# MLP input split beside the merge's output tiles, norm roots behind the up products, one ring of weight parts

## The reference, cut to what matters

```
x = x + g1 * merge_branches(ya, yb, pg, up_a, up_b, out_w)
#   merge: (sigmoid(pg_a) * (ya @ up_a) + sigmoid(pg_b) * (yb @ up_b)) @ out_w
x = x + g2 * squared_relu_mlp(modulate(rms_norm_2(x, norm2_w), sh2, sc2), mlp_w1, mlp_w2)
#   modulate(v, sh, sc) = v * (1 + sc) + sh
#   squared_relu_mlp(h, w1, w2) = square(relu(h @ w1)) @ w2          w1: 2048 x 8192
return rms_norm_2(x, final_norm_w)
```

## Time and profile before

| what | value |
|---|---|
| median of 3 runs | 4190.42 us |
| profiled execution: its time, its span | 4188.9 us, 4186.9 us |
| TensorE busy | 3830.8 us, 91% of the span |
| VectorE, ScalarE, GpSimd busy | 2062.7 (49%), 1522.9 (36%), 1636.1 us (39%) |
| mean granted TensorE clock, as a share of 2.4 GHz | 0.952 |
| HBM traffic | 139 GB/s over the span |
| stage C, first to last matmul | 3199.8 to 3392.7 us |
| up and down products of stage M | 3403.3 to 4173.0 us |

### The profile page before, as it was taken

The page is one execution under the profiler, slowest core; times in us unless marked ns, Lnnn a source line. Parts: engine busy times, 40 slices in busy tenths (PEclk is TensorE's granted clock), DMA queues, the critical chain, the costliest instruction groups (busy, mean ns, idle before and its releaser), DMA issues. The chain is left out here.

```text
span 4186.9 us, 86156 instructions
## 1 busy us (share of the span) xinstructions
PE 3830.8 (91%) x37360; PEld 3518.3 (84%) x37360; DVE 2062.7 (49%) x3724; ACT 1522.9 (36%) x2656; POOL 1636.1 (39%) x1160
## 2 busy tenths in 40 slices
PE   7898999898899899999879888898898979999998
PEld 6788887788888788888768778787787979999998
DVE  2544433533334677677665555556554443333333
ACT  3333343333344442232223333333333444444443
POOL 1544553444454553333311111111113636666664
PEclk9999998999999999999979999999997989999999
DMA  4354443344443677778500000000004535555553
GB/s 159 131 183 150 167 177 133 130 171 151 152 161 141 205 270 266 252 253 291 193 22 20 25 25 25 6 22 25 6 2 157 192 111 186 181 182 182 189 181 134
DMA packets 115670, 587.20 MB, mean 140 GB/s; under 512 B 20832, under 2 KB 40160, under 8 KB 50528
## 3 DMA queue, kind: packets, MB, share of 16 engines
q1 hardware_dynamic: 115296, 581.71, 39.0%
HBM read 560.95 MB, written 20.71 MB: 139 GB/s over the span
## 5 line engine op out<-in xcount | busy, mean ns | idle before, releaser
L536 PE MATMUL bank<-act_L,part_L 128*128 128x256 f32 x7296 | 968.5, 292 | 1.9 <-DVE act_L L1975 1.9
L536 PEld LDWEIGHTS bank<-act_L,part_L 128*128 128x128 f32 x7296 | 922.7, 197 | 36.9 <-issue 27.5
L2879 POOL TENSOR_TENSOR part_L<-wring,part_L 128x512 fp32r<-128x512 f32 x304 | 531.8, 1750 | 682.4 <-ACT part_L L1286 682.0
L536 PE MATMUL bank<-act_P,part_P 128*128 128x512 f32 (+1 forms) x3488 | 715.2, 365 | 18.2 <-POOL part_P L2879 12.7
L536 PEld LDWEIGHTS bank<-act_P,part_P 128*128 128x128 f32 x3488 | 590.2, 188 | 137.1 <-DVE arena_P L2342 16.3
L536 PE MATMUL bank<-arena_B 64*64 64x64 f32 (+3 forms) x13472 | 588.6, 230 | 43.6 <-DVE arena_B L2533 18.8
L536 PEld LDWEIGHTS bank<-arena_B 64*64 64x64 f32 (+2 forms) x13472 | 530.8, 143 | 97.4 <-DVE arena_B L2533 19.5
L2879 POOL TENSOR_TENSOR part_M<-wring,part_M 128x512 fp32r<-128x512 f32 x256 | 457.4, 1798 | 310.4 <-ACT part_M L1286 310.4
L1970 DVE TENSOR_TENSOR part_L<-wring,part_L 128x512 fp32r<-128x512 f32 x304 | 220.8, 727 | 517.7 <-ACT part_L L1286 517.7
L2879 POOL TENSOR_TENSOR part_P<-wring,part_P 128x512 fp32r<-128x512 f32 x184 | 307.3, 1676 | 430.1 <-ACT part_P L1286 430.1
L1286 ACT ACTIVATE part_L<-wring 128x1024 fp32r<-128x1024 f32 x304 | 320.3, 1054 | 293.2 <-PE bank L536 276.7
(11 more groups left out here) (252 smaller groups left out, 4013.6 us busy)
## 6 DMA issues: line engine op xcount, KB each, us to landing
wring<-in_w SPq DMA_DIRECT2D x404, 1024.0 KB, 4.8
arena_P<-in_w SPq DMA_DIRECT2D x64, 1024.0 KB, 4.9
mring<-in_w SPq DMA_DIRECT2D x32, 1024.0 KB, 5.2
z_kept<-arena_P SPq DMA_DIRECT2D x34, 256.0 KB, 5.6
z_kept<-arena_P SPq DMA_DIRECT2D x58, 128.0 KB, 5.9
xT<-z_kept SPq DMA_DIRECT2D x26, 256.0 KB, 2.8
arena_C<-z_kept SPq DMA_DIRECT2D x32, 128.0 KB, 3.0
cst<-z_kept SPq DMA_DIRECT2D x24, 128.0 KB, 2.4
```

The costliest lines, as they stand in the source:

```text
L536: return e.matmul(out, lhsT, rhs, start=start, stop=stop)
L2879: e.tensor_tensor(wl[:, 4:8, :], wring[s % NS][:, 8 * j + 4:8 * j + 8, :], wh[:, 4:8, :].bitcast(F32), sub).then_inc(*mark("pool_lo", "lop ...
```

## The change

What it does, part by part:

1. **One ring of parts.** Stage M's parts are stage C's; half h of M follows as half 64+h of C. The end and begin of stages between C and M are gone, and so is the separate start of the splits.
2. **Input split beside the output tiles.** `Z.h` is no longer the finished input, but only xT * A, split in high (ScalarE, one `cp` with a scale per partition) and low (VectorE, one instruction of xT, A and the high part), in `rest` of the next output tile. It takes the place of `K.y`, `Z.u` that of `K.act`.
3. **The shift as an extra column.** `Z.h` has 258 columns: column 256 (and 257) holds the shift. An up product has then 258 columns: x * A * W in 256 of them and shift * W in column 256.
4. **Roots behind the up product.** VectorE copies column 256 of the bank to `Z.bias` and multiplies the 256 columns by `Z.rb` (`up_scale`, in `ev`). ScalarE does relu with `Z.bias` added and then Square, rounding to `Z.u` high (`up_square`, in `ev`). VectorE squares once more for itself and subtracts (`up_low`), now in `rest` of the next tile, between the two splits of halves.
5. The sums of squares, the root and its spreading are done beside up tiles 0 and 1; up tile 0 is scaled in `rest` of tile 1.

```diff
-            K.act = acts("act_C", st)
-            K.y = acts("act_Y", st)
+            part["C"] = part["M"] = parts("C", st)
+            K.act = Z.u = acts("act_C", st)
+            yh_ = sb("act_Y", 32 * 258, FR, st)
+            K.y = yh_[:, 0:8192].rearrange("p (k s t) -> p k s t", k=16, s=2)
+            Z.h = yh_.rearrange("p (k s t) -> p k s t", k=16, s=2)
...
 tensor: project
-                    o = b[:, 256 * j:256 * j + 256] if apart else b[:, 0:256]
+                    o = b[:, 256 * j:256 * j + 256] if apart else b[:, 0:X.shape[-1]]
 tensor: mlp
+                    yield from project(
+                        "M", 32 * q + c, Z.h, ("th2",),
+                        (lambda: spread_norm(("M", 0), NR, small(1))) if (q, c) == (0, 1) else None,
+                        late=(lambda: add_squares(("M", 0), bs, K.sq[:, 15 % 4, :], 15)) if (q, c) == (0, 0) else None)
...
 scalar
+            def high_h2(c):
+                square(("M", 0), K.sq, c, ("x", 3, c), 4)
+                w.wait_ge(done("pj", "C", 15))
+                w.wait_ge(done("A", 2))
+                cp(Z.h[:, c, 0, 0:256], xT[:, c, :], A_[:, 2, c:c + 1]).then_inc(*mark("act_x", "h2h", c))
...
+            def up_square(q, c):
+                n = 16 * q + c
+                r = Z.tr[n % 3]
+                w.wait_ge(done("ur", n))
+                af(r, r, ACT.Relu, bias=Z.bias[:, n % 3:n % 3 + 1]).then_inc(*mark("act_tail"))
+                w.wait_ge(last("act_tail"))
+                w.wait_ge(done("pj", "M", 32 * q - 1) if q else done("pj", "C", 31))
+                af(Z.u[:, c, 0, :], r, ACT.Square).then_inc(*mark("act_x", "uh", q, c))
 scalar: mlp, ev of an up tile
-                        af(Z.tr[n % 3], b[:, 0:256], ACT.Relu).then_inc(*mark("act_tail", "free", "pj", u))
-                        w.wait_ge(done("usq", n))
-                        cp(Z.u[:, c, 0, :], Z.tr[n % 3]).then_inc(*mark("act_x", "uh", q, c))
+                            up_square(q, c)
 scalar: the seam
-            for h in range(lead("M")):
-                split("M", h)
-            spread_out(("M", 0), NR, Z.rb)
-            for k in range(16):
-                w.wait_ge(done("h2", k))
-                af(Z.tr[k % 3], Z.tr[k % 3], ACT.Identity, bias=mod[:, 48 + k, 0:1]).then_inc(*mark("act_x"))
-                w.wait_ge(last("act_x"))
-                cp(Z.h[:, k, 0, :], Z.tr[k % 3]).then_inc(*mark("act_x", "h2h", k))
...
 vector
+            def low_h2(c):
+                w.wait_ge(done("h2h", c))
+                own("dve_x")
+                stt(Z.h[:, c, 1, 0:256], xT[:, c, :], A_[:, 2, c:c + 1], Z.h[:, c, 0, 0:256].bitcast(F32), mult, sub)...
+            def up_scale(q, c, b, u):
+                n = 16 * q + c
+                w.wait_ge(done("pj", "M", 32 * q + c))
+                w.wait_ge(done("rb", ("M", 0)))
+                own("dve_tail")
+                own("dve_x")
+                e.tensor_copy(Z.bias[:, n % 3:n % 3 + 1], b[:, 256:257]).then_inc(*mark("dve_tail"))
+                tt(Z.tr[n % 3], b[:, 0:256], Z.rb, mult).then_inc(*mark("dve_tail", "free", "pj", u))
+                counts.at[("ur", n)] = counts.last("dve_tail")
+            def up_low(q, c):
+                r = Z.tr[(16 * q + c) % 3]
+                w.wait_ge(done("uh", q, c))
+                tt(r, r, r, mult).then_inc(*mark("dve_tail"))
+                own("dve_tail")
+                low(Z.u, c, r, "u", q, c)
 vector: mlp
+                    def rest(c=c):
+                        if (q, c) == (0, 0):
+                            low_h2(15)
+                        elif (q, c) == (0, 1):
+                            up_scale(0, 0, *first[0])
+                        elif c:
+                            up_low(0, 0) if (q, c) == (0, 2) else None
+                            up_low(q, c - 1)
+                    yield from project("M", 32 * q + c, ev, rest)
...
-                    yield from project("M", 32 * q + 16 + c, ev)
+                    yield from project("M", 32 * q + 16 + c, ev, (lambda: up_low(q, 15)) if c == 0 else None)
 gpsimd
+            weave.run(tail("M", 0, 1))
             root(("M", 0), small(1), 2)
-            for h in range(lead("M")):
-                split("M", h)
-            for q in range(4):
-                weave.run(tail("M", 32 * q, 32 * q + 32))
+            weave.run(tail("M", 1, 128))
```

More of the change, by code:

```diff
@@ L436, in program @@
         with ExitStack() as st:
[L437 to L440 removed]
+            part["C"] = part["M"] = parts("C", st)
[3 more added lines that the diff above has]
+            Z.h = yh_.rearrange("p (k s t) -> p k s t", k=16, s=2)
+            alloc, _, _ = arena("arena_C", 10500, st)
             K.mg = alloc(4096).rearrange("p (k t) -> p k t", k=16)
@@ L444, in program @@
             K.sq = alloc(1024).rearrange("p (r t) -> p r t", r=4)
[L445 to L449, removed]
+            Z.bias = alloc(4)
             Z.sq = alloc(2048).rearrange("p (r t) -> p r t", r=8)
@@ L634, in spread_norm @@
             def spread_norm(tag, ring, sm, step=1):
+                w.wait_ge(done("root", tag))
                 b, u = ring.take()
@@ L1265, in tensor @@
             weave.run(merges())
[L1266 to L1270, removed]
+            bs = open_norm(NR)
+            weave.run(out_c(bs))
             for q in range(4):
-                weave.run(mlp(q))
+                weave.run(mlp(q, bs))
             w.wait_ge(done("root", ("F", 1)))
@@ L1288, in split @@
             def split(stage, h):
-                if h >= sum(x[0] == "split" and x[1] == stage for x in TILES) * 2:
+                if stage == "C" and h >= 64:
+                    stage, h = "M", h - 64
+                if (stage, h) not in tile_of:
                     return
@@ L1295, in split @@
                     w.wait_ge(done("half", stage, h - NP[stage]))
+                elif stage == "M":
+                    w.wait_ge(done("half", "C", 64 + h - NP["C"]))
                 cp(part[stage][h % NP[stage]][0], wring[s % NS][:, 8 * j:8 * j + 8, :]).then_inc(*mark("act_hi", "hi", stage, h))
@@ L1901, in merges @@
                 mg_high(15)
-            def out_c():
[L1904 to L1910, removed]
+            def high_h2(c):
[3 more added lines that the diff above has]
+                cp(Z.h[:, c, 0, 0:256], xT[:, c, :], A_[:, 2, c:c + 1]).then_inc(*mark("act_x", "h2h", c))
@@ L1919, in ev @@
-                        cp(Z.u[:, c, 0, :], Z.tr[n % 3]).then_inc(*mark("act_x", "uh", q, c))
-                    yield from project("M", 32 * q + c, ev)
+                        if c == 0:
+                            w.wait_ge(done("pj", "C", 15))
+                            cp(Z.h[:, :, 0, 256:258], bcl(mod[:, 48:64, 0], 2)).then_inc(*mark("act_x", "shh"))
+                    yield from project("C", 16 + c, ev, (lambda c=c: high_h2(c - 1)) if c else None)
+            def up_square(q, c):
[6 more added lines that the diff above has]
+                af(Z.u[:, c, 0, :], r, ACT.Square).then_inc(*mark("act_x", "uh", q, c))
@@ new lines, in mlp, with ev @@
+            def mlp(q, bs):
+                for c in range(16):
+                    def ev(b, u, c=c):
+                        if (q, c) == (0, 0):
+                            sums_out(("M", 0), NR, bs, small(0), 15)
+                        else:
+                            up_square(q, c)
+                    def rest(c=c):
+                        if (q, c) == (0, 0):
+                            high_h2(15)
+                        if (q, c) == (0, 1):
+                            spread_out(("M", 0), NR, Z.rb)
+                            up_square(0, 0)
+                    yield from project("M", 32 * q + c, ev, rest)
@@ L2818, in ev, with rest @@
                     def ev(b, u, c=c):
[L2819 to L2826, removed]
+                        if (q, c) == (0, 0):
+                            first.append((b, u))
+                            mean(("M", 0), small(0), small(1))
+                        else:
+                            up_scale(q, c, b, u)
+                    def rest(c=c):
+                        if (q, c) == (0, 0):
+                            low_h2(15)
[4 more added lines that the diff above has]
+                            up_low(q, c - 1)
+                    yield from project("M", 32 * q + c, ev, rest)
                 for c in range(16):
@@ L2845, in vector @@
             weave.run(out_c())
-            ends("dve", "C")
-            begins(w, "C")
-            mean(("M", 0), small(0), small(1))
-            for h in range(lead("M")):
-                split("M", h)
[L2851 to L2858, removed]
+            first = []
             for q in range(4):
```

28 lines of the change are left out of this document (11 added, 17 removed).

## The result

| | median us | runs | against before |
|---|---|---|---|
| before | 4190.11 | 4188.5 to 4191.14 | |
| changed kernel | 4210.32 | 4209.08 to 4211.78 | 1.0049 (1.0031 to 1.0066) |

Slower by 20.2 us, where 25 were forecast. The profiled execution took 4211.78 us, its span is 4209.8.

A forecast was written before the change was run, and what follows sets the result against it. TensorE was taken to bound stage C and 728 us of stage M, with a seam of small steps between. -35.5 + 2.5 + 50 + 8 = +25 us on the profiled 4188.9 gave 4213.9, as median 4215 us, range 4188 to 4232.

The forecast's parts named there:

- extra columns: Up tiles of stage M: 258 columns instead of 256 make a tile 5.80 us instead of 5.76, +2.5 us.
- Step 1, the seam: Between C's last output tile and up tile 1 of M: 12.47 us in place of 47.98, -35.5 us.
- the walk: Times of splits and root after T, the end of C, against when they are wanted: nothing is late.
- Step 2: Output tiles of C: extra ScalarE and VectorE work, VectorE's sum 3.4 of 6.18 us, hidden by TensorE, costing nothing.
- Step 3, the loop: Up tiles of M: VectorE and GpSimd take turns, 6.58 us a tile against TensorE's 5.80; +50 us in four quarters.
- the rival of one wait: Up tiles: one VectorE wait for GpSimd, loop 5.1 to 5.7, TensorE bounds, 4157 us; 0.13 together with the rival's other case.
- The rival's other case: Up tiles: a half-closed loop of 6.0 to 6.2 us, 4175 to 4185 us; 0.13 together with the rival of one wait.
- Step 4, the clock: Behind the gap before block 15 in down tile 0: lower clock loses 2.0 us, between 0 and 3.4; +8 us.

The follow-up runs named there:

- low_before_split: Changed kernel with VectorE's square and low part of an up tile moved ahead of its split of the next half: 4154.48 us, 0.9916 of before.
- low_first_256: As low_before_split, but up products have 256 columns, without the shift's columns, so the values are not the MLP's: 4151.17 us, 0.9908 of before.
- square_first_low_behind: Changed kernel with only VectorE's square moved ahead of its split of the next half, the low part staying behind it: 4184.61 us, 0.9989 of before.
- gap_filled: Changed kernel with 44 unused matmuls of 256 columns in each down tile 0, ahead of its wait for block 15: 4201.47 us, 1.0029 of before.
- scalar_split_first: Changed kernel with ScalarE's up_square of a tile moved behind its split of the next half: 4153.55 us, 0.9910 of before.
- gpsimd_writes_only: Changed kernel with GpSimd's subtraction in stage M replaced by a memset of the same output, making values coarser: 4155.24 us, 0.9918 of before.

## Why the prediction was right

The direction and the mechanism held, the time lies 5 us from the forecast and in the range. By its terms, in us of D:

| term | forecast | measured |
|---|---|---|
| seam | -35.5 | -35.5 (12.49 for 47.98) |
| extra columns | +2.5 | 0 |
| loop, four quarters | +50 | +49.8 |
| clock behind the gap | +8 | +6.8 |
| sum | +25 | +20.9 |

The loop is D of the changed kernel less D of low_before_split, 56.6, less the clock's 6.8. These measured terms add to 21.1; the 0.2 left over is in tiles whose distances differ by some hundredths and in the reading of the seam's end.

**Step 1, the seam**, held: each time of the walk that I can read in the trace is within 0.2 us (GpSimd's root ended at T+6.7, forecast T+6.6). **Step 2** held: low parts beside the output tiles were held to about 1.4 us and TensorE paid nothing for them.

The extra columns are the term that was mis-sized. The rate of 0.42 ns a column was near: low_first_256 gives 0.36, 2.2 us in 64 tiles. But the base wasn't right: I took 120.0 ns for 256 columns in whatever layout, and in the new layout of rows of 258 they take 119.3, so that the two extra columns fill what the layout gave back. That the two cancel is chance.

**Step 3, the loop.** Six of its seven stations are within 0.05 us of the timeline: 0.47 for 0.52, split at 2.45 for 2.49, GpSimd's first end at 4.28 for 4.33, square 4.57 for 4.61, GpSimd's second 5.72 for 5.77, low part 6.00 for 6.05; the seventh, the next `up_scale`, is at 6.52 for 6.58. The term came out better than its parts. Loop (6.58) and TensorE's tile (5.80) were both forecast about 0.05 too long, and only their difference counts: 0.78 forecast, 0.77 measured. TensorE's wait from about tile 8 of a quarter came as said, too.

What was weak is the rival of one wait, "with one wait the loop is 5.1 to 5.7". square_first_low_behind is that case and came to 6.20, because the turn passes to the next VectorE instruction with two SBUF inputs. The rival's other case, a loop of 6.0 to 6.2 at 4175 to 4185, has the price that this kernel showed (6.20, 4184.6), but no instruction order behind it. Had the change left one wait, I would have forecast 4157 and been 28 us off.

**Step 4, the clock**, was right in kind, and 1.2 us too high. The measured loss, shown by gap_filled, is 2.2, 1.8, 1.5 and 1.4 us in the four quarters, where I took 2.0 each. The 2.0 was a choice inside bounds, and that it came so near is in part luck. In quarter 0 TensorE worked at the lower clock for 4.75 us of the window shown above and not for 3.4, but its matmuls started every 0.216 us there (22 in 4.75), less than twice the 0.119 of the window behind (164 in 19.5).

That seam and loop can be priced apart is shown by low_before_split, scalar_split_first and gpsimd_writes_only: they take the loop away by way of three different engines and leave the same D of 744.61.

## What to carry to other kernels

Walk the new order once around, from an instruction back to itself one tile later, and compare that length with the bounding engine's tile: busy shares of 52% on VectorE and 38% on GpSimd hid a loop of 113%. Where VectorE and GpSimd share work, count GpSimd's instructions inside the loop: in the three slow loops here each one held the next VectorE instruction with two SBUF inputs to its end, and moving a held instruction out of the way lets the next one wait (square_first_low_behind got back 25.5 of the 56.6 us); let the loop's steps run while GpSimd has nothing to do, or start GpSimd before the loop gets there. Buffers make a steady loss show late: the first eight tiles of a quarter ran at full speed, and about half of the loss was paid in the later tiles, the rest in one gap at the end, with the lower clock on top.

## What the runs showed of the hardware

- Matmuls of 256 float32r columns start every 120.0 ns when the rows of the moving operand lie 256 elements apart, and every 119.3 ns when they lie 258 apart (tiles of 5.76 and 5.73 us); 258 columns at 258 take 120.0. I know of no reason; other distances weren't tried.
- Behind the gap of 5.38 us, at a granted clock of 0.50, these matmuls started every 0.216 us (22 in 4.75 us).
- VectorE instructions with two SBUF inputs and GpSimd's subtractions took turns, each waiter next, in every order tried. The VectorE one ended 0.28 us (256 columns) or 0.54 us (512) behind GpSimd's end.
- A GpSimd memset of 128 by 512 took 0.53 us inside a VectorE subtraction of two SBUF operands, unhindered, and a VectorE instruction of two SBUF operands begun inside a memset took its 0.43 us (one case). A GpSimd subtraction of the same size took 1.29 us where nothing held it (the shortest in stage C of the kernel before) and 1.8 behind VectorE's split.
- A VectorE product with one operand in PSUM took 0.42 us inside a GpSimd subtraction, and 0.41 with GpSimd at rest (line 2853 at 3460.47 in the changed kernel).
